# Encoder layer: a third of the adaLN modulation ahead of the projections, the rest during attention

## Chip, core and metric

The kernel runs on one core of one Trainium2 chip. The metric is the device time of one execution in microseconds (us), the median of three runs. A profile is one further execution, recorded by the hardware. Engines are named as the profile names them: PE multiplies matrices (PEld loads its weights), DVE is the vector engine, ACT the scalar engine, POOL the general one, SP issues transfers; a "q" behind a name is the queue of that engine, where transfers (DMAs) are issued.

## What is computed

One bidirectional encoder layer over two sequences, a prompt of 256 tokens and a sample of 1024, width 1024. Each sequence has a vector `c`, from which six rows of 1024 are made that shift, scale and gate the two halves of the layer:

```python
mod = jax.nn.silu(c) @ w_ada + b_ada            # w_ada: 1024 x 6144, float32, 24 MB
sh1, sc1, g1, sh2, sc2, g2 = split(mod, 6)
u = layer_norm(x) * (1 + sc1) + sh1             # needs the first third of mod
h = u @ w_in                                    # then two attention groups, 8 + 8 heads
mix = concat(rms(o_a), rms(o_m)) @ w_out
x = layer_norm(alpha * x + g1 * mix, ...)       # from here on: the other two thirds
u2 = layer_norm(x) * (1 + sc2) + sh2
y = layer_norm(alpha * x + g2 * ffn(u2), ...)
```

The products of `mod` are plain float32 matmuls; nearly all others take their operands split into a high and a low part of type fp32r and sum three products (helper `three`, lines 158 to 160).

## The kernel before

Every instruction stands in its engine's stream in an order written out by hand, and engines wait for each other by semaphores. The stages that matter here follow one another:

`modulation` (from line 162). `w_ada` comes in 12 chunks of 512 columns, 2 MB each, into a ring of three (`w_ada_ring`, issued by SP, line 204). PE multiplies each chunk by `silu_c` in 8 steps, with 2 weight columns (one for each sequence), into a PSUM bank (line 224). DVE adds the bias (`mod_chunk`, line 260), and ACT stores the chunk to the DRAM tensor `mod_rows` (line 241). Beside it the projection weights arrive: 11 pieces (8 of `w_in`, 2 of `w_uq`, 1 of `w_ukv`), which POOL loads into a ring of two (`w_raw`, line 213), ACT rounds to the high part (line 238) and DVE subtracts for the low part (`split`, line 250). DVE takes one `split` and one `mod_chunk` in turn, and POOL loads piece m only after the split of piece m - 2.

`projections` is in the same block, so each engine goes on when its own stream allows. SP first waits for the first chunks of `mod_rows` and reads the columns of `sc1` and `sh1` back (`mod_in_t`, line 362), then loads the first two tiles of x and the tables. DVE takes the moments of two tiles (lines 640, 641), adds one to the scale (line 647) and makes `x_hat` (lines 655, 658). ACT and DVE overwrite memory of the stage before only after `after_modulation`: all 11 splits done, and all 12 chunks stored.

`attention` works through 16 heads of 9 units. In each unit PE does the scores of 128 keys against up to 1024 queries (lines 983, 984 for the first 8 heads, three products at 986 to 988 for the others), two matmuls for the maxima of a later head (line 1031) and the value products of the unit two back (`LAG = 2`). ACT takes the exponential (line 1084) and rounds it (line 1088), DVE makes the low part (line 1123) and the maxima (line 1131). The maxima, their transposes and those of the outputs share one pair of PSUM banks, `A_PAIR`, in an order that a list of `uses` numbers: each use waits until DVE has freed the one before (`a_free`). From head 8 on, `w_out` is split into `k.wo` high and low; until then these 64 KB in each partition are empty.

`output` and `channel` (the feed-forward part) read the other thirds of `mod_rows` later, from 838 us on.

Of the kernel before, what the change touches and what calls it, by code (L numbers as in the profile page):

```python
# [27 lines left out]
P = 128  # L28
# [41 lines left out]
class Kernel:  # L70
    def __init__(self, nc, ctx, ins, outs):
        self.nc, self.ctx = nc, ctx
        self.i, self.o = ins, outs
        self.names = set()

    def sem(self, name):
        return self.ctx.enter_context(self.nc.semaphore(name))
# [8 lines left out]
def encoder_layer(nc, ins, outs):  # L86
    ctx = ExitStack()
    with ctx:
# [3 lines left out]
        k.eps = k.sb(ctx, "eps", [P, 1])  # L92

# [13 lines left out]
        k.o_sample = lambda t: outs["y_sample"][0, t * P:(t + 1) * P, :]  # L107
        with ExitStack() as weights:
            k.win = [k.sb(weights, f"w_in_{s}", [P, KT, W_IN], F32R) for s in ("hi", "lo")]
            k.wuq = [k.sb(weights, f"w_uq_{s}", [P, RQ // P, HM * DM], F32R) for s in ("hi", "lo")]  # L110
            k.wukv = [k.sb(weights, f"w_ukv_{s}", [P, HM * (NOPE + VD)], F32R) for s in ("hi", "lo")]
            with nc.Block() as block, ExitStack() as early:
                k.early = early
                with ExitStack() as stage:
                    modulation(k, stage, block)
                with ExitStack() as stage:
                    projections(k, stage, block)
        k.u2_memory = ctx.enter_context(ExitStack())
        with ExitStack() as weights:
            w_out_lo_memory = weights.enter_context(ExitStack())  # L120
            k.wo = [k.sb(weights, "w_out_hi", [P, KT, D], F32R), k.sb(w_out_lo_memory, "w_out_lo", [P, KT, D], F32R)]
            with ExitStack() as stage:
                attention(k, stage)

            k.u2 = [k.sb(k.u2_memory, f"u2_{s}", [P, KT, TOK], F32R, side="right") for s in ("hi", "lo")]
# [38 lines left out]
def modulation(k, stage, block):  # L164
# [4 lines left out]
    NC = 6 * D // 512  # L169
    RING = 3  # L170
    right = lambda name, shape: k.sb(stage, name, shape, side="right")
    c_t = right("c_t", [P, KT, 2])
    silu_c = right("silu_c", [P, KT, 2])
    wa = right("w_ada_ring", [P, RING, KT, 512])
    bias = right("b_ada_rows", [2, 6 * D])
    mrow = right("mod_chunk", [2, 2, 512])
    raw = right("w_raw", [P, 2, W_IN])
    c_in, ident_in = k.sem("c_in"), k.sem("ident_in")
    wa_in = [k.sem(f"wa_in{s}") for s in range(RING)]
    b_in = k.sem("b_ada_in")  # L180
    raw_in = [k.sem(f"raw_in{s}") for s in range(2)]
    c_ready, mod_done, mod_sum = k.sem("c_ready"), k.sem("mod_done"), k.sem("mod_sum")
    mod_out = [k.sem(f"mod_out{s}") for s in range(2)]
# [7 lines left out]
    k.mod_out, k.lo_done, k.pieces = mod_out, lo_done, len(pieces)  # L191
    k.ident_in, k.eps_ready = ident_in, k.sem("eps_ready")

    @block.sync
    def _(sp):
# [4 lines left out]
        wsrc = k.i["w_ada"][0].rearrange("(p j) n -> p j n", j=KT)  # L200
        for n in range(NC):
            if n >= RING:
                sp.wait_ge(mod_done, n - RING + 1)
            sp.dma_start(wa[:, n % RING, :, :], wsrc[:, :, n * 512:(n + 1) * 512]).then_inc(wa_in[n % RING], 16)

    @block.gpsimd
    def _(pool):
        pool.memset(k.eps[:, :], EPS).then_inc(k.eps_ready, 1)
        pool.dma_start(k.ident[:, :], k.i["ident"]).then_inc(ident_in, 16)
# [6 lines left out]
    @block.tensor  # L216
    def _(pe):
        pe.wait_ge(c_ready, 1)
        for n in range(NC):
            pe.wait_ge(wa_in[n % RING], 16 * (n // RING + 1))  # L220
            if n >= 8:
                pe.wait_ge(mod_sum, n - 7)
            for j in range(KT):
                mm = pe.matmul(bank(k, n % 8)[0:2, :], silu_c[:, j, :], wa[:, n % RING, j, :],  # L224
                               start=j == 0, stop=j == KT - 1)
            mm.then_inc(mod_done, 1)

    @block.scalar
    def _(act):
        act.dma_start(bias[:, :], k.i["b_ada"][0, :].partition_broadcast(2)).then_inc(b_in, 16)  # L230
        act.wait_ge(c_in, 32)
        act.activation(silu_c[:, :, :], c_t[:, :, :], ACT.Silu).then_inc(c_ready, 1)
        assert len(pieces) <= NC
        for n in range(NC):
            if n < len(pieces):
                act.wait_ge(raw_in[n % 2], 16 * (n // 2 + 1))
                hi = pieces[n][1]
                act.activation(hi, raw[:, n % 2, :hi.shape[-1]], ACT.Copy).then_inc(hi_done, 1)
            if n >= 1:
                act.wait_ge(mod_sum, n)  # L240
                act.dma_start(k.mod[:, (n - 1) * 512:n * 512], mrow[:, (n - 1) % 2, :]).then_inc(mod_out[(n - 1) % 2], 16)
        act.wait_ge(mod_sum, NC)
        act.dma_start(k.mod[:, (NC - 1) * 512:], mrow[:, (NC - 1) % 2, :]).then_inc(mod_out[(NC - 1) % 2], 16)

    @block.vector
    def _(dve):
# [4 lines left out]

        for n in range(NC):
            if n < len(pieces):
# [4 lines left out]
            if n >= 2:  # L258
                dve.wait_ge(mod_out[n % 2], 16 * (n // 2))
            dve.tensor_tensor(mrow[:, n % 2, :], bank(k, n % 8)[0:2, :], bias[:, n * 512:(n + 1) * 512], ALU.add).then_inc(mod_sum, 1)  # L260
        for m in range(NC, len(pieces)):
# [4 lines left out]
def projections(k, stage, block):  # L266
# [54 lines left out]
    tabs_in, mod_in, modp = k.sem("tabs_in"), k.sem("mod_in"), k.sem("mod_plus_one")  # L321
# [34 lines left out]
    def _(sp):  # L356
        for s in range(2):
            sp.wait_ge(k.mod_out[s], 32)
        with nc.allow_non_contiguous_dma(reason="modulation columns, once"):
            for s in range(2):  # L360
                for m, part in enumerate((1, 0)):
# [116 lines left out]
    def _(act):  # L478
# [22 lines left out]
        for n in TURNS:  # L501
            a, b, c = n - 1, n - 3, n - 4
            if n < NT:
                if n == 0:
                    act.wait_ge(modp, 1)
# [118 lines left out]
    def _(dve):  # L624
# [20 lines left out]
        dve.wait_ge(mod_in, 64)  # L645
        for s in range(2):
            m = dve.tensor_scalar(modt[:, s, 0, :], modt[:, s, 0, :], 1.0, None, ALU.add)
            if s == 0:
                link(m)
        m.then_inc(modp, 1)  # L650
# [112 lines left out]
def attention(k, stage):  # L763
# [31 lines left out]

    q_in, k_in, v_in = ([k.sem(f"{n}{s}") for s in range(RING)] for n in ("q_in", "k_in", "v_in"))
# [44 lines left out]
    for g in range(H):  # L841
        for u in range(UNITS):
# [4 lines left out]
            if beside(g, u):  # L847
                uses.append(("item", *beside(g, u)))
    uses.append(("outputs", H - 1))
# [8 lines left out]
    def out_use(g):  # L858
        return number["outputs", g]

# [56 lines left out]
    with nc.Block() as block:  # L917
        @block.sync
        def _(sp):
            load_first(sp)  # L920

            for g in range(H):
                sp.wait_ge(m_row, g + 1)
                row = qs[1][DA:DA + 1, g % RING, :] if gqa(g) else qs[0][DM:DM + 1, g % RING, :]
                sp.dma_start(row.bitcast(F32), mrow[:, :].bitcast(F32)).then_inc(m_in, 16)

        @block.gpsimd
        def _(pool):
# [21 lines left out]
            with nc.allow_non_contiguous_dma(reason="columns of gains, once"):  # L950
                for m, name in enumerate(("grp_norm_a", "grp_norm_b")):
                    pool.dma_start(gain[:, 4 * m:4 * m + 4], k.i[name][0, :].rearrange("(j p) -> p j", p=P)).then_inc(gain_in, 16)
            for g in range(H):
# [9 lines left out]
        def _(pe):  # L963
# [81 lines left out]

            for i in range(ITEMS):
# [4 lines left out]
            for g in range(H):  # L1051
                for u in range(UNITS):
# [15 lines left out]
                    if beside(g, u) and twice:  # L1068
                        maxima(*beside(g, u))
            for u in range(UNITS - LAG, UNITS):  # L1070
# [4 lines left out]
        def _(act):  # L1075
# [24 lines left out]
            def w_out_hi(j):  # L1100

                act.wait_ge(gain_in, 32)
                act.wait_ge(wo_in, 16 * (j + 1))
                act.activation(k.wo[0][:, j, :], wo_raw[:, :], ACT.Copy, scale=gain[:, j:j + 1]).then_inc(wo_hi, 1)

            for g in range(H):
                for u in range(UNITS):
                    exp(g, u)
                    if u == 1 and g >= 1:
# [8 lines left out]
        def _(dve):  # L1118
# [39 lines left out]

            for i in range(ITEMS):
# [4 lines left out]
            for g in range(H):  # L1164
                for u in range(UNITS):
# [7 lines left out]
                    if beside(g, u):  # L1173
                        maximum(*beside(g, u))
                    if u == 8 and g >= HA:
# [762 lines left out]
```

## Time and profile before

| | |
|---|---|
| median of three runs | 1982.06 us (1980.81 to 1983.81) |
| profiled execution | 1981.43 us, its span from first to last instruction 1979.6 us |
| PE busy | 1807.0 us, 91% |
| DVE busy | 1163.6 us, 59% |
| ACT busy | 697.9 us, 35% |
| modulation | to 98.8 us |
| projections | about 99 to 364 us |
| attention | 364 to about 820 us |

Busy shares over the span average stages with different limits, so each stage is read by itself below. The end of a matmul is modelled in the records, and a matmul's record overlaps the next one's; what it costs in a stream is the distance between two starts. A plain float32 matmul leaves two records, so 96 instructions of line 224 are x192.

### The profile page before, as it was taken

Reading aid. Unit: us, or ns where it says so; the run is one execution under the profiler, and the core shown is the slowest. Engines: PE = TensorE matmul, PEld = TensorE weight load, DVE = VectorE, ACT = ScalarE, POOL = GpSimd, SP = SyncE. Lnnn points to the kernel's source line nnn. Section 1 sums busy time; section 2 is a strip of 40 time slices with the busy share of each in tenths; the row PEclk is TensorE's granted clock in tenths of the full one; section 3 lists DMA queues with packets and bytes.
Section 4 is the critical chain, followed back from the end, with each engine's and each line's share of the span. In section 5 each row is a group of like instructions: output and inputs, shape, how many; then the busy total and the mean of one; then the engine's idle time right before and its main releaser. Section 6 shows DMA issues by size and latency. Waiting matters only on the chain. (4 is left out here: it accounts for less than half of the span.)

```text
span 1979.6 us, 22389 instructions
## 1 busy us (share of the span) xinstructions
PE 1807.0 (91%) x8558; PEld 1395.8 (71%) x8558; DVE 1163.6 (59%) x1406; ACT 697.9 (35%) x1081; POOL 210.2 (11%) x218
## 2 busy tenths in 40 slices
PE   7989896399999999679979999999999999999993
PEld 1188885266667777467768888888888888888873
DVE  1268887488887777359854434434444434444488
ACT  1145654277776766534431111111111111111114
POOL 0012333111022221000000000000000000000053
PEclk9989997699999999889989999999999999999997
DMA  9913435713155543143241111111111111111133
GB/s 348 323 57 91 133 108 157 173 46 77 46 120 135 123 105 80 47 138 107 75 128 32 33 42 32 32 53 32 32 42 32 32 53 32 32 42 32 34 105 128
DMA packets 145001, 171.56 MB, mean 87 GB/s; under 512 B 21434, under 2 KB 108506, under 8 KB 144930
## 3 DMA queue, kind: packets, MB, share of 16 engines
q1 hardware_dynamic: 130352, 121.72, 19.7%
q0 software_dynamic: 12016, 46.22, 9.3%
q10 hardware_dynamic: 2564, 2.72, 0.5%
q8 instruction: 42, 0.69, 0.1%
q14 instruction: 27, 0.22, 0.0%
HBM read 128.22 MB, written 42.32 MB: 86 GB/s over the span
## 5 line engine op out<-in xcount | busy, mean ns | idle before, releaser
L1796 DVE TENSOR_TENSOR sum_f<-pair,sum_f 128x1024 f32<-128x1024 f32 x200 | 244.1, 1221 | 468.5 <-PE pair L160 466.8
L158 PE MATMUL pair<-u_hi,w_out_hi 128*128 128x512 f32 (+1 forms) x1056 | 377.0, 357 | 12.2 <-DVE w_out_hi L1424 12.2
L160 PE MATMUL pair<-u_hi,w_out_hi 128*128 128x512 f32 (+1 forms) x1056 | 374.9, 355 | 0.0
L159 PE MATMUL pair<-u_lo,w_out_hi 128*128 128x512 f32 (+1 forms) x1056 | 372.4, 353 | 0.0
L1644 ACT ACTIVATE silu_gate<-pair 128x512 f32<-128x512 f32 (+1 forms) x63 | 33.2, 526 | 574.9 <-PE pair L160 574.9
L158 PEld LDWEIGHTS pair<-u_hi,w_out_hi 128*128 128x128 f32 x1056 | 199.1, 189 | 40.0 <-DVE w_out_hi L1424 12.4
L160 PEld LDWEIGHTS pair<-u_hi,w_out_hi 128*128 128x128 f32 x1056 | 199.0, 188 | 31.1
L159 PEld LDWEIGHTS pair<-u_lo,w_out_hi 128*128 128x128 f32 x1056 | 198.7, 188 | 30.4
L1123 DVE TENSOR_TENSOR p_lo<-p_f,p_hi 128x1024 fp32r<-128x1024 f32 (+1 forms) x144 | 167.2, 1162 | 43.4 <-ACT p_hi L1088 42.9
L158 PE MATMUL pair<-down_hi,hidden_hi 128*128 128x512 f32 x440 | 183.2, 416 | 9.6 <-DVEq L1767 6.1
L1084 ACT ACTIVATE p_f<-pair 128x1024 f32<-128x1024 f32 (+1 forms) x144 | 140.6, 977 | 141.9 <-PE pair L984 69.4
L1131 DVE TENSOR_REDUCE max_col<-pair 128x1 f32<-128x1024 f32 x128 | 155.7, 1221 | 57.3 <-PE pair L1031 57.2
L160 PE MATMUL pair<-down_hi,hidden_lo 128*128 128x512 f32 x440 | 173.5, 394 | 0.0
L159 PE MATMUL pair<-down_lo,hidden_hi 128*128 128x512 f32 x440 | 172.6, 392 | 0.0
L1088 ACT ACTIVATE p_hi<-p_f 128x1024 fp32r<-128x1024 f32 (+1 forms) x144 | 145.8, 1012 | 4.6
L1536 POOL TENSOR_TENSOR sum_f<-sum_f,gate 128x1024 f32<-128x1024 f32 x10 | 29.9, 3015 | 878.3 <-DVE sum_f L1796 878.3
L158 PEld LDWEIGHTS pair<-down_hi,hidden_hi 128*128 128x128 f32 x440 | 82.9, 188 | 56.1 <-DVE sum_f L1796 33.0
L1031 PE MATMUL pair<-k_a,q_a 128*128 128x512 f32 (+3 forms) x288 | 94.2, 412 | 29.7 <-DMA k_a<-ka_t_hi_rows 20.9
L158 PE MATMUL pair<-p_hi,v_hi 128*65 128x512 f32 (+1 forms) x288 | 111.7, 388 | 2.5 <-ACT o_t L1095 1.0
L159 PE MATMUL pair<-p_lo,v_hi 128*65 128x512 f32 (+1 forms) x288 | 109.7, 381 | 0.0
L160 PE MATMUL pair<-p_hi,v_lo 128*65 128x512 f32 (+1 forms) x288 | 109.7, 381 | 0.0
L224 PE MATMUL pair<-w_ada_ring,silu_c 128*2 128x512 f32 x192 | 84.3, 602 | 14.5 <-DMA w_ada_ring<-in_w_ada 14.5
(236 smaller groups left out, 2935.0 us busy)
## 6 DMA issues: line engine op xcount, KB each, us to landing
w_ada_ring<-in_w_ada SPq DMA_DIRECT2D x12, 2048.0 KB, 12.5
gate_up_raw<-in_w_gate SPq DMA_DIRECT2D x21, 512.0 KB, 4.0
gate_up_raw<-in_w_up SPq DMA_DIRECT2D x21, 512.0 KB, 5.2
down_raw<-in_w_down SPq DMA_DIRECT2D x21, 512.0 KB, 3.2
o<-o_head POOLq DMA_DIRECT2D x16, 320.0 KB, 3.6
o_tile<-o SPq DMA_DIRECT2D x10, 512.0 KB, 4.1
x<-y SPq DMA_DIRECT2D x10, 512.0 KB, 2.6
gate_up_raw<-x SPq DMA_DIRECT2D x10, 512.0 KB, 3.6
```

What stands on the lines that cost most here:

```text
L158: pe.matmul(out, a[0], b[0], start=start, stop=False)
L159: pe.matmul(out, a[0], b[1], start=False, stop=False)
L160: return pe.matmul(out, a[1], b[0], start=False, stop=stop)
L224: mm = pe.matmul(bank(k, n % 8)[0:2, :], silu_c[:, j, :], wa[:, n % RING, j, :], start=j == 0, stop=j == KT - 1)
L1031: mm = pe.matmul(dst, qs[0][0:w, s, q], ks[0][0:w, n, key], start=True, stop=True)
L1084: act.activation(pf[:, c % PS, 0:w], src, ACT.Exp, scale=scale).then_inc(e_done, 1)
L1088: act.activation(ph[0][:, c % PS, 0:w], pf[:, c % PS, 0:w], ACT.Copy).then_inc(p_hi, 1)
L1123: dve.tensor_tensor(ph[1][:, c % PS, 0:w], pf[:, c % PS, 0:w], ph[0][:, c % PS, 0:w], ALU.subtract).then_inc(p_lo, 1)
L1131: dve.reduce_max(mcol[:, NTP + i:NTP + i + 1], a_pair(m)[:, :, :].rearrange("p a b -> p (a b)"), AX.X).then_inc(a_free, 1)
L1536: pool.tensor_tensor(sumf[:, t, :], sumf[:, t, :], g2[:, int(t >= NTP), :], ALU.mult).then_inc(gated, 1)
L1644: act.activation(sg[:, 0:hi - lo], k.bank[(slot + c + 1) % 2][:, 0, 0:hi - lo], ACT.Silu).then_inc(silu_done, 1)
L1796: dve.tensor_tensor(sumf[:, t, :], src, sumf[:, t, :], ALU.add).then_inc(dn_added, 1)
```

## The change

1. `modulation` keeps 4 of the 12 chunks (`NC = 2 * D // 512`), each with its own buffer. SP issues chunks 0 and 1, then the first two tiles of x, then chunks 2 and 3, then the tables.
2. The columns of `sc1` and `sh1` no longer go through DRAM. PE transposes each finished chunk, four pieces of 2x128 into bank 7 (`columns`), one chunk behind the products; DVE copies them to `modt`, adding one to the scale. `after_modulation` waits for the splits and for these two copies.
3. DVE does up to three splits ahead of each chunk's sum: 0 to 2, sum 0, 3 to 5, sum 1, 6 to 8, sum 2, 9 and 10, sum 3. ACT rounds the 11 pieces without stores in between.
4. The other 4096 columns come during attention in 16 loads of 1 MB that ACT issues, one in every third unit (heads 0 to 2, then late in head 3 to head 5), into the empty memory of `k.wo`. In unit 2 of head 3 and unit 2 of head 7 PE does 32 plain float32 matmuls each (`modulate_late`), with 32 weight columns (2 of `silu_c` and 30 zeros); the four blocks of 512 columns go to the four groups of 32 PSUM partitions of one bank. DVE adds the bias in one instruction, SP stores the rows.
5. POOL adds a memset and 8 small loads of the bias at the start of attention. SP clears the semaphores of the first two stages (63 by my count) at the start of attention, behind its first loads.

```diff
@@ modulation, SP, PE and DVE
-        for n in range(NC):
-            if n >= RING:
-                sp.wait_ge(mod_done, n - RING + 1)
-            sp.dma_start(wa[:, n % RING, :, :], wsrc[:, :, n * 512:(n + 1) * 512]).then_inc(wa_in[n % RING], 16)
+        for n in range(2):
+            load_first(sp, n)
+        def columns(n):
+            pe.wait_ge(mod_sum, n + 1)
+            for q in range(4):
+                at = 2 * (4 * n + q)
+                mm = pe.transpose(bank(k, 7)[:, at:at + 2], mrow[:, n, q * P:(q + 1) * P], k.ident[0:2, 0:2])
+            mm.then_inc(k.mod_tr, 1)
...
+            if n >= 1:
+                columns(n - 1)
+        columns(NC - 1)
+        done = 0
         for n in range(NC):
-            if n < len(pieces):
-                split(n)
+            for m in range(done, min(done + 3, len(pieces))):
+                split(m)
+            done += 3
             dve.wait_ge(mod_done, n + 1)
@@ projections, waits, SP and DVE
         eng.wait_ge(k.lo_done, k.pieces)
-        for s in range(2):
-            eng.wait_ge(k.mod_out[s], 16 * (6 * D // 512 // 2))
+        eng.wait_ge(modp, 2)
-                    sp.dma_start(modt[:, s, m, :], k.mod[s, part * D:(part + 1) * D].rearrange("(j p) -> p j", p=P)).then_inc(mod_in, 16)
         for t in range(2):
             sp.dma_start(xt[:, t, :], xrow(k, t)).then_inc(x_in[t], 16)
+        for n in (2, 3):
+            k.load_w_ada(sp, n)
+        dve.wait_ge(k.mod_tr, 4)
+        cols = bank(k, 7)[:, 0:4 * KT].rearrange("p (m j s) -> p m s j", m=2, s=2)
+        dve.tensor_copy(modt[:, :, 1, :], cols[:, 0, :, :]).then_inc(modp, 1)
+        dve.tensor_scalar(modt[:, :, 0, :], cols[:, 1, :, :], 1.0, None, ALU.add).then_inc(modp, 1)
@@ attention
+    LATE_AT = {(3, 2): 0, (7, 2): 1}
+    LATE_LOADS = {}
+    for half, (g0, u0) in enumerate(((0, 2), (3, 5))):
+        for j in range(KT):
+            c = g0 * 9 + u0 + 3 * j
+            LATE_LOADS[c // 9, c % 9] = (half, j)
...
+            for done in k.first:
+                sp.sem_clear(done)
...
+            def modulate_late(half):
+                use_before(pe, late_use(half))
+                pe.wait_ge(late_in, 16 * KT * (half + 1))
+                for j in range(KT):
+                    for q in range(4):
+                        mm = pe.matmul(A_PAIR[32 * q:32 * q + 32, 0, :], k.silu_c[:, j, :], late_w[:, j, q * 512:(q + 1) * 512],
+                                       start=j == 0, stop=j == KT - 1)
+                mm.then_inc(a_ready, 1)
...
+            def load_late(half, j):
+                if half == 1:
+                    act.wait_ge(a_ready, late_use(0) + 1)
+                at = FIRST + HALF * half
+                act.dma_start(late_w[:, j, :], k.wada[:, j, at:at + HALF]).then_inc(late_in, 16)
...
+            def late_sum(half):
+                dve.wait_ge(a_ready, late_use(half) + 1)
+                dve.wait_ge(late_b_in, 16 * 8)
+                dve.tensor_tensor(late_row[:, half, :], A_PAIR[:, 0, :], late_bias[:, half, :], ALU.add).then_inc(a_free, 1)
```

## Rows read from the trace of the kernel before

**Rows 1.** Busy time by stretch; columns as in the first line, clock and DMA share last.
```profile
core 0: us, PE busy (x) PEld busy (x) DVE busy (x) ACT busy (x) POOL busy (x), PEclk, DMA share, GB/s
2.00:98.70 96.70, 84.23 (x192) 16.42 (x192) 20.80 (x22) 12.98 (x13) 5.87 (x12) 1.00 0.97 343
40.00:80.00 40.00, 40.00 (x94) 7.89 (x93) 10.99 (x12) 6.44 (x6) 2.68 (x5) 1.00 1.03 386
104.00:120.00 16.00, 13.63 (x63) 12.46 (x63) 7.75 (x13) 8.89 (x21) 0.00 (x0) 0.70 0.29 100
385.00:565.00 180.00, 173.35 (x796) 118.47 (x795) 146.56 (x155) 127.46 (x141) 23.24 (x35) 0.97 0.29 65
590.00:791.00 201.00, 200.25 (x954) 143.97 (x953) 159.82 (x167) 139.60 (x153) 41.85 (x63) 1.00 0.45 109
```

**Rows 2.** The modulation products: group by line, first and last records, and DVE's sums.
```profile
L224 PE MATMUL pair<-w_ada_ring,silu_c 128*2 128x512 f32 x192 | 84.3, 602 | 14.5 <-DMA w_ada_ring<-in_w_ada 14.5
14.47 45.69 PE L224 MATMUL pair<-w_ada_ring,silu_c 128*2 128x512 f32 x102 [14.47 <-DMA w_ada_ring<-in_w_ada]
17.84 0.13 PEld L224 LDWEIGHTS pair<-w_ada_ring,silu_c 128*2 128x2 f32 x1 [0.73 <-issue]
23.29 0.68 DVE L260 TENSOR_TENSOR mod_chunk<-pair,b_ada_rows 2x512 f32<-2x512 f32 x1 [13.19 <-PE pair L224]
30.16 0.68 DVE L260 TENSOR_TENSOR mod_chunk<-pair,b_ada_rows 2x512 f32<-2x512 f32 x1 [4.89 <-PE pair L224]
```

**Rows 3.** The path of a weight piece, in order of time: POOL's load, ACT, DVE.
```profile
2.00 1.07 POOL L213 DMA_DIRECT2D w_raw<-in_w_in  x2
7.51 1.17 ACT L238 ACTIVATE w_in_hi<-w_raw 128x1184 fp32r<-128x1184 f32 x1
8.71 1.39 DVE L250 TENSOR_TENSOR w_in_lo<-w_raw,w_in_hi 128x1184 fp32r<-128x1184 f32 x1 [8.71 <-ACT w_in_hi L238]
25.57 0.53 POOL L213 DMA_DIRECT2D w_raw<-in_w_in  x1 [14.63 <-DVE w_in_lo L250]
33.33 1.19 ACT L238 ACTIVATE w_in_hi<-w_raw 128x1184 fp32r<-128x1184 f32 x1 [7.84 <-DMA w_raw<-in_w_in]
66.77 0.54 POOL L213 DMA_DIRECT2D w_raw<-in_w_uq  x1 [6.33 <-DVE w_in_lo L250]
72.80 0.84 ACT L238 ACTIVATE w_uq_hi<-w_raw 128x768 fp32r<-128x768 f32 x1 [6.08 <-DMA w_raw<-in_w_uq]
73.20 0.54 POOL L213 DMA_DIRECT2D w_raw<-in_w_ukv  x1 [5.89 <-DVE w_uq_lo L250]
80.51 1.06 ACT L238 ACTIVATE w_ukv_hi<-w_raw 128x1024 fp32r<-128x1024 f32 x1 [6.86 <-DMA w_raw<-in_w_ukv]
85.70 1.20 DVE L250 TENSOR_TENSOR w_ukv_lo<-w_raw,w_ukv_hi 128x1024 fp32r<-128x1024 f32 x1
```

**Rows 4.** From the last chunk to the first projection product, in order of time.
```profile
98.83 0.68 DVE L260 TENSOR_TENSOR mod_chunk<-pair,b_ada_rows 2x512 f32<-2x512 f32 x1 [6.19 <-PE pair L224]
100.99 1.37 DVE L640 BATCH_NORM_STATS2 x_stats<-x_tile 128x6 f32<-128x512 f32 x2
102.78 0.16 DVE L655 RECIPROCAL x_std<-x_std 128x1 f32<-128x1 f32 x1
110.45 0.69 PE L158 MATMUL pair<-w_in_hi,u_hi 128*128 128x384 f32 x1 [1.23 <-DVE u_lo L744]
```

**Rows 5.** PE's groups in heads 0 to 7 (390 to 565 us); last: idle before, by releaser.
```profile
L983 PE MATMUL pair<-q_a,k_a 128*128 128x512 f32 (+1 forms) x124 | 48.3, 392 | 0.0
L1031 PE MATMUL pair<-k_a,q_a 128*128 128x512 f32 (+2 forms) x124 | 40.4, 408 | 4.5 <-DVE max_col L1131 4.1
```

**Rows 6.** SP from the start of attention, in order of time; last, 8 issues merged.
```profile
368.71 5.43 SPq L915 DMA_DIRECT2D v_lo<-va_lo_rows  x1
384.24 180.31 SPq L925 DMA_DIRECT2D q_b<-neg_max_row  x8
```

**Rows 7.** Prices of an issue and of a register move on a queue: min, median, max ns.
```profile
L1334 ACTq DMA_DIRECT2D gate_up_raw<-in_w_up x1: 596/596/596, 994.5 to 994.5; - x1
L241 ACTq DMA_DIRECT2D mod_rows<-mod_chunk x11: 229/230/246, 24.0 to 92.7; - x11
L1507 SPq MOVE gate_up_raw<-in_w_gate x20: 29/29/35, 1033.6 to 1837.0; - x20
```

**Rows 8.** Who waited for whom in attention, 385 to 565 us: total, times, longest.
```profile
POOL q_a L883 <- PE pair L984: 76.5, 6, 42.2
ACT p_f L1084 <- PE pair L984: 60.6, 42, 25.9
DVE p_lo L1123 <- ACT p_hi L1088: 13.3, 26, 1.0
```

**Rows 9.** DVE's maxima in heads 0 to 7, 385 to 565 us; columns as in rows 5.
```profile
L1131 DVE TENSOR_REDUCE max_col<-pair 128x1 f32<-128x1024 f32 x57 | 69.6, 1221 | 16.7 <-PE pair L1031 16.6
```

More of the change, by code:

```diff
@@ L73, in __init__ @@
         self.i, self.o = ins, outs
-        self.names = set()
+        self.sems, self.first = ctx, []
     def sem(self, name):
-        return self.ctx.enter_context(self.nc.semaphore(name))
+        found = self.sems.enter_context(self.nc.semaphore(name))
+        if self.sems is not self.ctx:
+            self.first.append(found)
+        return found
     def sb(self, stage, name, shape, dt=F32, side=None):
@@ L189, in modulation, with load_first @@
     pieces += [(k.i["w_ukv"][0], k.wukv[0][:, :], k.wukv[1][:, :])]
-    k.mod_out, k.lo_done, k.pieces = mod_out, lo_done, len(pieces)
+    k.lo_done, k.pieces = lo_done, len(pieces)
     k.ident_in, k.eps_ready = ident_in, k.sem("eps_ready")
+    k.wada = k.i["w_ada"][0].rearrange("(p j) n -> p j n", j=KT)
+    def load_first(sp, n):
+        sp.dma_start(wa[:, n, :, :], k.wada[:, :, n * 512:(n + 1) * 512]).then_inc(wa_in[n], 16)
+    k.load_w_ada = load_first
     @block.sync
@@ L208, in _ @@
         pool.memset(k.eps[:, :], EPS).then_inc(k.eps_ready, 1)
+        pool.memset(k.silu_c[:, :, :], 0.0).then_inc(c_zero, 1)
         pool.dma_start(k.ident[:, :], k.i["ident"]).then_inc(ident_in, 16)
@@ L217, in _ @@
     def _(pe):
+        def columns(n):
[4 more added lines that the diff above has]
+            mm.then_inc(k.mod_tr, 1)
         pe.wait_ge(c_ready, 1)
+        pe.wait_ge(ident_in, 16)
         for n in range(NC):
-            pe.wait_ge(wa_in[n % RING], 16 * (n // RING + 1))
-            if n >= 8:
-                pe.wait_ge(mod_sum, n - 7)
+            pe.wait_ge(wa_in[n], 16)
             for j in range(KT):
-                mm = pe.matmul(bank(k, n % 8)[0:2, :], silu_c[:, j, :], wa[:, n % RING, j, :],
-                               start=j == 0, stop=j == KT - 1)
+                mm = pe.matmul(bank(k, n)[0:2, :], k.silu_c[:, j, 0:2], wa[:, n, j, :], start=j == 0, stop=j == KT - 1)
             mm.then_inc(mod_done, 1)
+            if n >= 1:
+                columns(n - 1)
+        columns(NC - 1)
     @block.scalar
     def _(act):
-        act.dma_start(bias[:, :], k.i["b_ada"][0, :].partition_broadcast(2)).then_inc(b_in, 16)
+        act.dma_start(bias[:, :], k.i["b_ada"][0, 0:2 * D].partition_broadcast(2)).then_inc(b_in, 16)
         act.wait_ge(c_in, 32)
-        act.activation(silu_c[:, :, :], c_t[:, :, :], ACT.Silu).then_inc(c_ready, 1)
-        assert len(pieces) <= NC
-        for n in range(NC):
-            if n < len(pieces):
[L236 to L243, printed above, removed]
+        act.wait_ge(c_zero, 1)
+        act.activation(k.silu_c[:, :, 0:2], c_t[:, :, :], ACT.Silu).then_inc(c_ready, 1)
+        for n, (src, hi, lo) in enumerate(pieces):
+            act.wait_ge(raw_in[n % 2], 16 * (n // 2 + 1))
+            act.activation(hi, raw[:, n % 2, :hi.shape[-1]], ACT.Copy).then_inc(hi_done, 1)
     @block.vector
@@ L257, in _ @@
                 dve.wait_ge(b_in, 16)
[L258 to L261, printed above, removed]
+            dve.tensor_tensor(mrow[:, n, :], bank(k, n)[0:2, :], bias[:, n * 512:(n + 1) * 512], ALU.add).then_inc(mod_sum, 1)
+        for m in range(done, len(pieces)):
             split(m)
@@ L859, in out_use, with late_use @@
         return number["outputs", g]
+    def late_use(half):
+        return number["late", half]
     def a_pair(m):
@@ L925, in _ @@
                 sp.dma_start(row.bitcast(F32), mrow[:, :].bitcast(F32)).then_inc(m_in, 16)
+                for (late_g, _), half in LATE_AT.items():
+                    if late_g == g:
+                        sp.wait_ge(a_free, late_use(half) + 1)
+                        for q in range(4):
+                            at = FIRST + HALF * half + 512 * q
+                            sp.dma_start(k.mod[:, at:at + 512], late_row[32 * q:32 * q + 2, half, :]).then_inc(late_out, 16)
+            sp.wait_ge(late_out, 16 * 8)
         @block.gpsimd
@@ L952, in _ @@
                     pool.dma_start(gain[:, 4 * m:4 * m + 4], k.i[name][0, :].rearrange("(j p) -> p j", p=P)).then_inc(gain_in, 16)
+            link(pool.memset(late_bias[:, :, :], 0.0))
+            for q in range(4):
+                for half in range(2):
+                    at = FIRST + HALF * half + 512 * q
+                    pool.dma_start(late_bias[32 * q:32 * q + 2, half, :], k.i["b_ada"][0, at:at + 512].partition_broadcast(2)).then_inc(late_b_in, 16)
             for g in range(H):
@@ L1108, in _ @@
                     exp(g, u)
+                    if (g, u) in LATE_LOADS:
+                        load_late(*LATE_LOADS[g, u])
                     if u == 1 and g >= 1:
```

52 lines of the change are left out of this document (28 added, 24 removed).

## The prediction, made before the changed kernel ran

> **What bounds the kernel now.** I read busy time by stretch first, then the order of time at the front, then PE's groups in attention.
>
> The front. Until 98.7 us PE does nothing but the modulation products, 84.2 us of records at a granted clock of 1.00 (2.4 GHz), while the DMA engines are busy 0.97 of the stretch and 1.03 from 40 to 80 us [rows 1]. The reader is to see two resources that are both full: PE needs 30.16 - 23.29 = 6.87 us for a chunk [rows 2], and a chunk of 2.1 MB with a piece of 0.6 MB in 6.87 us is 393 GB/s, about what the stretch moved (386). Projections can't begin before both the weights and the modulation are there; the first product comes at 110.45 us, 11.6 us after the last chunk's sum [rows 4].
>
> Attention. PE is busy 173.4 of 180 us in heads 0 to 7 and 200.3 of 201 us later [rows 1], at a clock of 0.97 to 1.00. Its idle time is small (4.5 us in 175 us before the maxima [rows 5]), and ACT waits for PE more than for anything (60.6 us [rows 8]). So PE bounds attention too: whatever is added to PE's stream there lengthens it nearly one for one. PE is full where the products leave and full where they arrive, so moving them alone is worth nothing: the change gains only if they cost less PE time in attention than the front gets shorter.
>
> **The change part by part.** (a) The front. PE's share falls from 12 chunks to 4: first chunk from 14.47 to 23.29 us (its first records stand 0.86 apart, at the lower clock, the rest 0.43 [rows 2]), then three of 6.87 us, so PE alone would end at 23.3 + 20.6 = 43.9 us. The loads: four chunks and two x tiles are 9.4 MB on SP's queue, and pieces 0 to 6, some 4.2 MB, pass beside them; 13.6 MB at 380 GB/s from about 4 us on lands at 40 us, so the last chunk ends at about 47 us.
>
> The weight pieces take over as the limit. A slot of the ring turns in: issue to ACT's start 7.8 us (25.57 to 33.33), ACT 1.2, DVE 1.4, about 0.3 until the next issue, together 10.7 us with DMA busy and 5.5 + 2.9 = 8.4 us where it is not (2.00 to 7.51) [rows 3]. The w_uq pieces take 6.0 + 0.8 + 0.9 + 0.3 = 8.0, w_ukv 7.3 + 1.1 + 1.2 + 0.3 = 9.9 [rows 3]. Slot 0: split 0 ends at 10.1 us, then 20.5, 31, 41.5 for pieces 2, 4, 6, about 49 for piece 8 and 57 to 59 for piece 10, the last two lower by a microsecond or so each as the chunks are in by then. Slot 1: split 3 waits behind sum 0 and ends at 25.4, piece 5 at 36, 7 at 46, 9 at 54. I take 57 us for split 10. Sum 3 stands behind it on DVE, and sums 1 and 2 behind splits 5 and 8; who waits for them is only PE's transposes, and those of the last chunk are hidden under the moments. From sum 3 the tail is that of before: 98.83 to 102.78 is 3.95 us to the first reciprocal [rows 4], with two small copies (0.3 us) where the two additions were. So the reciprocal comes at 61 us in place of 102.8: **-42 us**. Best case, where every piece lands in 5.5 us, the last chunk decides: 47 + 4 = 51 us, -51; worst, every piece at 7.8 us and one more microsecond of waiting in each: 66 us, -37. The x tiles, 1 MB, cost nothing of their own: they are ahead of chunk 2 but inside the sum of loads. The read-back through DRAM was hidden behind chunks 10 and 11 and is worth nothing here. From the first reciprocal on, projections run as before, with the same dip of the clock (0.70 of 2.4 GHz from 104 to 120 us [rows 1]), since PE idles before them in both.
>
> (b) The products moved into attention. 64 instructions of 512 columns. At the front an instruction costs 6.87 / 8 = 0.859 us at the full clock, in two records 0.43 us apart [rows 2]. No row shows instructions that write different groups of 32 partitions one after another, so I bound them. One behind the other they cost 64 x 0.859 = **+55 us**. Each in its own quarter of the array with nothing shared they cost a quarter, **+13.7 us**. Between them: neighbours overlap, but the two passes of one instruction use the same quarter and, issued in order, hold back what stands behind them. Then the second pass of one runs beside the first pass of the next, and each instruction costs one pass, 0.43 us: **+27.5 us**. I take this one, because rows 2 show the two passes of an instruction always 0.43 us apart, one after the other, and because the order in which they are issued is fixed by the program. A gain below a quarter is excluded: there are four groups.
>
> No row bears on whether the array can do it. The Trainium skill, TensorEngine Tiling (Array Packing), Key Properties, says that different tiles load weights and multiply in parallel, and its table promises up to 4x for 32 columns. The Trainium skill, TensorE: Matmul & The Clock Gate, Measured speedup vs the span model, gives 2.38x for three column tiles (as an estimate, 3.1x for four, 18 us here, a sum of 1961); the same page's section The mechanism says that matmuls start and end strictly in program order, which is what would hold back the second pass. No run shown so far says which.
>
> (c) Around each burst. PE first waits for DVE to free A_PAIR; the value products between hide the maximum's 1.22 us [rows 9]. DVE sits in its wait for the burst with the next low part and maximum queued behind; PE needs that low part only two units on, after scores, maxima and values (a unit is 180.3 / 63 = 2.9 us of PE work, seven heads by nine units [rows 6], against DVE's 0.7 + 1.2 us). ACT starves during the burst, but it isn't the bound. I put 1 us to a burst, **+2 us**; the bounds are 0 and 3 each.
>
> (d) ACT's 16 issues. 0.23 us for a tiny one, 0.60 for 512 KB [rows 7]; with 0.5 us, 8 us of ACT in heads 0 to 5. ACT is busy 127 of 180 us there [rows 1], and a low part is needed two units later, so most hides: **+1 us**, between 0 and 9 (all exposed). The loads add 16 MB in some 150 us (51 units) to a stretch at 65 GB/s and 0.29 busy, far from full; head loads are issued two heads ahead, and POOL's waits there are for PE [rows 8].
>
> (e) At nothing: POOL's memset and 8 small loads (some 6 us, and POOL's next task waits up to 42 us for PE [rows 8]); DVE's two sums of 0.7 us; SP's stores; w_out's later wait, which is over by head 8. SP's 63 clears stand behind its first loads and ahead of the first row of maxima: SP is free from 374.1 to 384.24 us [rows 6] (its row there ends at 368.71 + 5.43), 160 ns for each. The cheapest rows are 29 ns for a move and 230 ns for a small issue [rows 7]: 0 us by the first, 4 by the second; I take 0, as a clear moves no data.
>
> The sum: -42 + 27.5 + 2 + 1 = -11.5 us. The profiled span of 1979.6 becomes 1968.1, with 1.8 us around it 1969.9 (its own time was 1981.43). The median of the runs shown is 0.6 us above that: **1970.5 us**.
>
> **The rivals.** Full overlap: the four groups run side by side, 13.7 us in place of 27.5: 1956.7 us. For it: pass and weight load of another quarter share nothing that a row shows. Against: it needs PE to pass over an instruction that waits.
>
> No overlap, the one that ends slower: the 32-column instructions queue one behind the other like those with 2 columns, each burst is 27.5 us, and PE's full stream in attention is 55 us longer: -42 + 55 + 3 = +16, 1998 us. It decides from the point where an instruction costs more than (42 - 3) / 64 = 0.61 us. For it: every stream of the trace shows starts one behind the other; also that a 2-column product costs the same per column as any. Against: no stream of before has neighbours in different groups, so none could show it. This is also the case in which the change doesn't do what it says, since the work is only moved.
>
> Front not shortened as summed: pieces and clears at their bad ends together (-37, +4, and ACT's +9): 1984.5 with the half overlap, no change.
>
> **How the numbers follow.** Half overlap 0.40, full 0.30, none 0.25, bad ends together 0.05. The range has to reach the none case, since leaving it out leaves more than 2 in 10 out: 1950 (full overlap, front at -49) to 2001 (none, with 3 us of the open costs). The likeliest case's own range is 1961 to 1979. A difference of 0.2%, 4 us, is about what a measurement of this kernel can tell from no change. Faster 0.70, same 0.05, slower 0.25.
>
> **What would show it.** In the profile after: the first `x_hat` at 57 to 66 us, with DVE's last split as what its sum stood behind, and DMA busy near 1.0 until about 40 us; the two bursts in heads 3 and 7 of 13.7 us each (7 for full overlap, 27.5 for none), seen as the distance between the starts of neighbouring records; the rest of attention as long as before, with heads 0 to 5 longer by less than 2 us; the first row of maxima 20 us after attention's start. Wrong would be: a burst that waits for its loads, a front that ends with the chunks and not with the pieces, or a clock that falls around the bursts, which I hold at 1.00 because PE never idles there.

## The result and the profile after

The changed kernel takes 1953.0 us (median of four runs, 1951.4 to 1953.3) against 1981.4 us for the kernel before beside it: a ratio of 0.985, 95% interval 0.983 to 0.986. It is 28 us faster, where 11.5 us was forecast. In the profiled executions the span falls from 1979.6 to 1951.5 us.

Busy time by stretch in the changed kernel (columns as in [rows 1]); the last line but one is heads 0 to 6 (as the line from 385 to 565 us in [rows 1] is), the last is a late part of attention:

```profile
span 1951.5 us, 22479 instructions
PE 1770.9 (91%) x8574; PEld 1391.4 (71%) x8574; DVE 1159.8 (59%) x1400; ACT 699.1 (36%) x1081; POOL 216.0 (11%) x228
0.00:40.00 40.00, 23.23 (x47) 4.35 (x48) 10.93 (x9) 9.83 (x9) 5.53 (x15) 0.96 0.96 351
58.04:75.26 17.22, 13.70 (x55) 12.56 (x56) 8.89 (x16) 9.04 (x22) 0.00 (x0) 0.60 0.26 92
345.00:525.00 180.00, 174.59 (x836) 117.77 (x837) 142.94 (x150) 124.78 (x139) 22.35 (x34) 0.97 0.53 154
550.00:751.00 201.00, 200.25 (x955) 143.49 (x952) 160.34 (x168) 139.75 (x152) 41.97 (x63) 1.00 0.45 109
```

PE does 36 us less in all (1807.0 before), although the same products of the modulation are made. DMA moves 154 GB/s in heads 0 to 6 in place of 65 [rows 1], half busy.

The front of the changed kernel in order of time; these lines answer to [rows 2 to 4]:

```profile
33.89 8.72 PE L242 MATMUL pair<-w_ada_first,silu_c 128*2 128x512 f32 x16 [2.07 <-DMA w_ada_first<-in_w_ada]
42.88 7.03 PE L242 MATMUL pair<-w_ada_first,silu_c 128*2 128x512 f32 x16
51.86 1.06 ACT L256 ACTIVATE w_ukv_hi<-w_raw 128x1024 fp32r<-128x1024 f32 x1 [1.87 <-DMA w_raw<-in_w_ukv]
52.95 1.22 DVE L263 TENSOR_TENSOR w_ukv_lo<-w_raw,w_ukv_hi 128x1024 fp32r<-128x1024 f32 x1 [1.96 <-ACT w_ukv_hi L256]
54.09 0.67 DVE L273 TENSOR_TENSOR mod_chunk<-pair,b_ada_rows 2x512 f32<-2x512 f32 x1
58.04 0.16 DVE L661 RECIPROCAL x_std<-x_std 128x1 f32<-128x1 f32 x1
65.70 0.69 PE L167 MATMUL pair<-w_in_hi,u_hi 128*128 128x384 f32 x1 [1.23 <-DVE u_lo L750]
```

The reader is to see that the product of the last chunk ends at 49.9 us (42.88 + 7.03), but its sum stands behind the last split on DVE, which ends at 54.2 us. The first reciprocal comes at 58.04 us. The last chunk's product stood behind the one before it, which took 8.72 us in place of 6.87: PE had waited 2.07 us for that chunk, and from 33.89 to 37.4 us its granted clock was 0.54. The splits end later still, so this costs nothing here.

A burst in attention, PE's products as one merged line, then the first weight loads (PEld), the next unit's first score and DVE's sum. A float32 product leaves two records, here called its passes, each with a weight load of its own; a quarter is the part of the array that writes one group of 32 PSUM partitions:

```profile
432.50 7.07 PE L1089 MATMUL pair<-w_ada_late,silu_c 128*32 128x512 f32 x64 [0.61 <-DVE max_col L1190]
432.50 0.16 PEld L1089 LDWEIGHTS pair<-w_ada_late,silu_c 128*32 128x32 f32 x8 [0.87 <-DVE max_col L1190]
432.96 0.13 PEld L1089 LDWEIGHTS pair<-w_ada_late,silu_c 128*32 128x32 f32 x4 [0.30 <-issue]
433.39 0.13 PEld L1089 LDWEIGHTS pair<-w_ada_late,silu_c 128*32 128x32 f32 x4 [0.30 <-issue]
439.51 0.50 PE L1021 MATMUL pair<-q_a,k_a 128*128 128x512 f32 x1
439.64 0.69 DVE L1222 TENSOR_TENSOR mod_late<-pair,b_ada_late 128x512 f32<-128x512 f32 x1 [7.20 <-PE pair L1089]
```

64 passes take 7.07 us. Eight weight loads come at the start and then four in each step of 0.43 us, not one: all four quarters of the array are at work. The granted clock is 1.00 throughout. The scores of the next unit begin at 439.51, and DVE's sum 7.2 us after its last work. The second burst, from 543.27 us, takes 7.07 us as well.

SP's issues place the stages: its first load of attention, and the rows of maxima, of which the merged line that begins with head 8's is the last (in the changed kernel the lines between, from head 4 on, are left out). First the kernel before, then the changed one:

```profile
364.34 0.51 SPq L913 DMA_DIRECT2D q_a<-qa_t_hi_rows  x1
589.69 201.99 SPq L925 DMA_DIRECT2D q_a<-neg_max_row  x8
```

```profile
321.19 0.51 SPq L937 DMA_DIRECT2D q_a<-qa_t_hi_rows  x1
341.09 77.21 SPq L951 DMA_DIRECT2D q_b<-neg_max_row  x4
561.69 201.96 SPq L951 DMA_DIRECT2D q_a<-neg_max_row  x8
```

| event | before, us | after, us | difference |
|---|---|---|---|
| first reciprocal | 102.78 | 58.04 | -44.7 |
| attention's first load | 364.34 | 321.19 | -43.15 |
| row of maxima, head 0 | 384.24 | 341.09 | -43.15 |
| row of maxima, head 8 | 589.69 | 561.69 | -28.0 |
| end of the span | 1979.6 | 1951.5 | -28.1 |

So the front gives 44.7 us, projections lose 1.6 of them, heads 0 to 7 lose 15.15, and nothing changes behind head 8.

### The profile page after: what moved, and what is told of

It is laid out like the page before. It is cut to its first block and busy times, and to the rows that moved or that the text cites. A ratio compares the mean times of both kernels' runs of the same rounds, so it can differ in the third digit from the quotient of the medians.

```text
span 1951.5 us, 22479 instructions
## 1 busy us (share of the span) xinstructions
PE 1770.9 (91%) x8574; PEld 1391.4 (71%) x8574; DVE 1159.8 (59%) x1400; ACT 699.1 (36%) x1081; POOL 216.0 (11%) x228
## 5 line engine op out<-in xcount | busy, mean ns | idle before, releaser
L169 PEld LDWEIGHTS pair<-down_hi,hidden_lo 128*128 128x128 f32 x440 | 82.8, 188 | 20.0
```

The lines of the kernel that those rows point to most:

```text
L169: return pe.matmul(out, a[1], b[0], start=False, stop=stop)
```

## The experiments

The question was why 64 products cost so little, so the first runs change only the order and the place of the late products. All runs below whose number of executions isn't given were timed in one execution; the kernel before, beside them, took 1981.6 us (four products in a row, 64 loads: 1981.9). Theory A was that of the prediction (issued in order, a product whose quarter is busy holds back all behind it), theory B that PE looks past it.

**All products of one quarter, then the next.**

```diff
-                for j in range(KT):
-                    for q in range(4):
+                for q in range(4):
+                    for j in range(KT):
```

> The 32 products of a burst in another order: all eight of one group of 32 PSUM partitions, then all eight of the next. Nothing else is changed and the result is the same. Theory A (issued in order, and a product whose quarter is busy holds back all behind it): neighbours in the stream share a quarter in 28 of 31 places, so a burst goes from 7.1 us to about 27 us and the span from 1951.5 to about 1992 us. Theory B (PE looks past a product that waits for its quarter, at least over some instructions): the burst stays near 7 us if it looks past 8 instructions, and lies between if it looks past fewer.

Measured: 1983.2 us, a span of 1981.4. The burst in order of time, and three of its weight loads:

```profile
431.09 22.59 PE L1089 MATMUL pair<-w_ada_late,silu_c 128*32 128x512 f32 x64 [0.61 <-DVE max_col L1190]
435.84 0.11 PEld L1089 LDWEIGHTS pair<-w_ada_late,silu_c 128*32 128x32 f32 x1 [0.32 <-issue]
436.27 0.14 PEld L1089 LDWEIGHTS pair<-w_ada_late,silu_c 128*32 128x32 f32 x3 [0.32 <-issue]
436.70 0.14 PEld L1089 LDWEIGHTS pair<-w_ada_late,silu_c 128*32 128x32 f32 x2 [0.29 <-issue]
```

22.6 us is neither 27 nor 7. The first quarter has 16 passes; 12 steps after the start (431.09 + 12 x 0.43 = 436.25) the loads become three and then two: the next quarter has begun, four passes before the first is through. Weight loads can stand ahead of their passes (eight at the start of the burst shown above, where four passes begin), so the loads alone would not prove it; the length of the burst does, 52.5 steps for 64 passes. PE looks ahead, but not far. The whole gain of the late products hangs on their order: in this one the changed kernel takes as long as the kernel before.

**Two products of a quarter in a row.** The loops are now over pairs of `j`, the quarter, and `j` within the pair.

> The 32 products of a burst with two of the same quarter in a row before the next quarter, result unchanged. Theory A (in order, a product whose quarter is busy holds back all behind it): of the four passes of a pair, only the last runs beside the next quarter's first, three passes of 0.43 us for a pair, 16 pairs, about 20 us for a burst and a span of about 1977 us. Theory B (PE looks past waiting products): 7 us and 1951.5 us.

Measured: 1951.5 us, a burst of 7.14 us. Theory A, by which four passes of one quarter in a row hold back the next, falls: it gave 20 us. The records show four passes begun within the first step (431.0 to 431.4 us), where the first four of the stream are all of one quarter. Since passes of one quarter take 0.43 us each one after another (the run with all products in one quarter, below), passes of other quarters must here have begun ahead of earlier ones that waited.

**Two weight columns in place of 32.**

```diff
-                        mm = pe.matmul(A_PAIR[32 * q:32 * q + 32, 0, :], k.silu_c[:, j, :], ...
+                        mm = pe.matmul(A_PAIR[32 * q:32 * q + 2, 0, :], k.silu_c[:, j, 0:2], ...
```

> The weights of the late products are 2 columns in place of 32 (the 30 zeros left out), in the same four groups of partitions. If the overlap comes from the group of partitions alone, the burst stays at 7.1 us and the span at 1951.5 us. If it needs 32 full columns, a burst takes 27.5 us and the span is about 1992 us.

Measured: 1955.6 us, a burst of 7.05 us. The overlap comes from the group of partitions; the 30 columns of zeros are not needed for it. Up to head 8 this run is as fast as the changed kernel (that row of maxima comes at 560.94 us); its span is 2.3 us longer, all of it behind that, where the two kernels do the same, so I don't put it down to the edit. Why this execution was longer there is not shown.

**All products in one quarter.**

```diff
-                        mm = pe.matmul(A_PAIR[32 * q:32 * q + 32, 0, :], ...
+                        mm = pe.matmul(A_PAIR[0:32, q % 2, :], ...
```

The `start` and `stop` marks are moved too, so that two groups of columns share a bank; these lines are left out here.

> All late products write partitions 0 to 31 (into two banks in turn), so that no two of them use different quarters; two thirds of the modulation are therefore not what they should be. Both theories: no overlap, 0.86 us for a product, 27.5 us for a burst, a span of about 1992 us, slower than the kernel before by 12 us. If the span stays near 1951.5, it isn't the quarters that make the burst short.

Measured: 1994.5 us, a span of 1992.7, a burst of 27.65 us:

```profile
431.13 27.65 PE L1089 MATMUL pair<-w_ada_late,silu_c 128*32 128x512 f32 x64 [0.61 <-DVE max_col L1190]
```

This is the rival without overlap, built: the change without its four groups would be slower than the kernel before by some 13 us. Four quarters make a burst 27.65 / 7.07 = 3.9 times shorter.

**Four products of a quarter in a row.** From the three orders so far (the change's, two and eight in a row) I fitted a rule: a pass begins once the pass four places ahead of it in the stream has begun and its own quarter is free. It gives 16 steps for the change's order and for two in a row, and 52 for eight in a row (52 x 0.43 = 22.4). The run was chosen because the rule had to say something new.

> Four products of a quarter in a row (eight passes), then four of the next, result unchanged. From the two orders run so far I take that PE begins a pass at most four passes ahead of the one that waits: eight products in a row took 22.6 us (52.6 steps of 0.43), two in a row 7.1. By that rule a quarter begins 4 steps after the one before, the second round too, so 36 steps: 15.5 us for a burst and a span of about 1968 us. If PE looked past eight passes it would be about 7 to 9 us (1953 us); if it looked past none, 24 us (1985 us).

Measured: 1970.6 us, a burst of 15.85 us against 15.5 by the rule, a span of 1968.8 against 1968. The rule held where it could have failed. It isn't the only one that fits: if each quarter takes up to four passes, the running one with them, and PE hands them out in order until one is full, the five orders need the same 16, 16, 36, 52 and 64 steps. The runs can't tell the two apart, and what in PE makes it four is not shown.

**Price of the products in place.** Of each burst only the first 4 of 32 products are left.

> Each late burst does only its first 4 of 32 products (28 left out, so two thirds of the modulation are wrong); loads, sums, stores and waits stay. It prices the products in place. A burst falls from 7.1 to about 0.9 us. If the products cost PE's stream their own length and nothing else, the time falls by 2 x 6.0 = 12 us from that of the changed kernel, to about 1941 us; if their neighbourhood (stalls behind them, a fall of the clock) costs more, by up to 18 us.

Measured: 1940.4 us (median of four; ratio to before 0.979, interval 0.977 to 0.980). From attention's first load to the row of head 8 it is 549.19 - 320.68 = 228.5 us, against 240.5 in the changed kernel and 225.35 before. So 56 products cost 12.0 us, 0.214 each, a quarter of 0.859, and nothing around them. Of the 15.15 us of heads 0 to 7, 13.7 are products; 1.4 are all the rest: two waits of 0.61 and 0.65 us for the maximum and what little else there is.

**Price of the loads.** In addition to the short bursts 14 of the 16 loads are left out (the wait for them is lowered to match; that line is left out here).

```diff
-        for j in range(KT):
+        for j in range(1):
             c = g0 * 9 + u0 + 3 * j
```

> As the run with short bursts, and 14 of the 16 loads during attention are left out too (what they bring is not used there). It prices ACT's issues, 0.33 us each in the profile of the changed kernel, and their 14 MB. If all is hidden, as theory has it, the time is that of the run with short bursts, 1941 us. If the issues are exposed, it is 14 x 0.33 = 4.7 us lower, 1936 us.

Measured: 1940.7 us (median of four), within 0.4 us of the run with the loads, and 548.82 - 320.12 = 228.7 us over the same stretch. The loads and their issues cost nothing that can be measured.

**64 loads of 256 KB.** How many issues can ACT's stream take?

> The 16 late loads of 1 MB cut into 64 of 256 KB, four issued by ACT in a row at the same places; result unchanged. ACT issues 48 more, some 16 us in heads 0 to 5, in lumps of 1.3 us. If there is room for them in ACT's stream, the span stays at 1951.5 us within 1; if the lumps reach PE through the low parts, it is up to 16 us longer, 1967 us.

Measured: 1956.1 us; from attention's first load to the row of head 8 244.7 us, 4.2 more than in the changed kernel. Who waited for whom on PE shows where:

```profile
PE pair L167 <- DVE p_lo L1184: 4.3, 4, 1.1
```

The line is of the stretch from 340 to 520 us (total, times, longest); in the same stretch of the changed kernel this wait doesn't appear. Four issues in a row in ACT's stream delay a rounding so far that PE's value products wait for the low part, four times for about a microsecond; the other lumps are hidden. One issue at a time, which took 0.33 us, has room.

The last runs ask what ends the front, and go beyond the change. The changed kernel was timed again beside the first two.

> The changed kernel itself, timed beside the next two: 1953 us, 0.985 of the kernel before.

Measured: 1952.3 us (median of five, as in all runs from here on), ratio 0.984 (0.983 to 0.986).

**The moments first.**

```diff
         moments(0)
         moments(1)
+        k.last_turn()
         dve.wait_ge(k.mod_tr, 4)
```

`k.last_turn` does splits 9 and 10 and sum 3; the loop that it is taken out of is left out here.

> The moments of the first two x tiles (3.3 us of DVE) stand behind sum 2 and ahead of splits 9 and 10 and sum 3, where DVE waits for pieces, in place of behind sum 3. If the front ends with the weight pieces and the tail behind them, the first reciprocal comes about 2.5 us sooner, at 55.5 us, and the time falls by 2 to 3 us, to about 1950.5 us. If something else ends it (the table load of ACT, the product of the last chunk), nothing moves.

Measured: 1950.0 us (ratio to before 0.983, interval 0.982 to 0.985). The first reciprocal comes at 53.91 us, where the changed kernel run beside it has 57.08. The intervals of the two ratios overlap; what the trace shows beyond doubt is the 3.2 us at the reciprocal.

**A third buffer for the pieces.**

```diff
+    third = k.xh[:, :, :].rearrange("p a b -> p (a b)")
+    def slot(m, w):
+        return third[:, 0:w] if m % 3 == 2 else raw[:, m % 3, 0:w]
...
-            if m >= 2:
-                pool.wait_ge(lo_done, m - 1)
+            if m >= 3:
+                pool.wait_ge(lo_done, m - 2)
```

> As the run with the moments first, and the weight pieces have a third buffer (in the memory of x_hat, which is free until then), so that a piece is loaded three ahead. If the ring of two limits the front, as my sum said, split 10 ends at about 49 us in place of 54.2, the last chunk's product at 50 us becomes the limit, and the reciprocal comes at about 52 us, 3 us sooner again: about 1947 us. If DMA bandwidth limits it, the pieces only take from the chunks, the last chunk lands later and little is won: 1950 us.

Measured: 1945.9 us (ratio 0.981, interval 0.980 to 0.982), and 1946.0 when timed again. The front of this run in order of time:

```profile
43.00 7.03 PE L248 MATMUL pair<-w_ada_first,silu_c 128*2 128x512 f32 x16 [1.77 <-DMA w_ada_first<-in_w_ada]
48.86 1.22 DVE L269 TENSOR_TENSOR w_ukv_lo<-w_raw,w_ukv_hi 128x1024 fp32r<-128x1024 f32 x1 [2.32 <-ACT w_ukv_hi L262]
50.07 0.68 DVE L277 TENSOR_TENSOR mod_chunk<-pair,b_ada_rows 2x512 f32<-2x512 f32 x1
51.41 0.15 DVE L668 RECIPROCAL x_std<-x_std 128x1 f32<-128x1 f32 x1
```

The last split (ends at 50.08) and the last product (50.03) now come together, so both limits of the front are met at once. The last chunk lands later than in the changed kernel, at 43.0 us in place of 40.8 (12.8 + 28.0 from issue to landing), and PE waits 1.77 us for it. That fits the expectation's rival, by which the pieces take from the chunks, but they give more than they take. This version beats both kernels: 6.4 us less than the changed one beside it (1952.3), 37.9 less than the kernel before.

**Spare products on PE.** Projections take 263.15 us from the first reciprocal to attention's first load, against 261.56 before. The granted clock of the first 17.2 us is 0.60 where the same stretch of before (102.78 to 120 us) has 0.70, and PE had idled from 49.9 to 59.2 us but for two groups of small transposes; before the change it idled 5.2 us. This run tests whether that is the cause.

```diff
         columns(NC - 1)
+        pe.wait_ge(lo_done, len(pieces))
+        k.keep_busy(pe, 8)
...
+                if n < 2:
+                    k.keep_busy(pe, 4 + 4 * n)
```

> As the run with three pieces, and PE does 20 spare fp32r products of 384 columns (into a bank that nobody reads) where it idles before the first projection products: 8 behind the last chunk, 4 and 8 behind the transposes of the first two tiles. In the changed kernel projections took 1.6 us longer from the first reciprocal to the end of the stage than before, beside a longer spell at half clock. If that spell is the cause, and PE's idling brings it, the spell shrinks, the first products come 0.17 us apart in place of 0.32, and the time falls by 1 to 3 us below the 1945.9 us of the run with three pieces. If the spell costs nothing (DVE is the limit there), or the spare products delay the transposes, the time stays or rises by up to 2 us.

> The run with three pieces again, beside the one with the spare products: 1946 us, 0.981 of the kernel before.

Measured: 1945.5 us (0.981, interval 0.980 to 0.983) beside 1946.0 for its base. The stretch from 51 to 64 us, first with the spare products, then without:

```profile
51.00:64.00 13.00, 11.38 (x69) 10.48 (x69) 5.60 (x12) 8.08 (x20) 0.00 (x0) 1.00 0.35 120
```

```profile
51.00:64.00 13.00, 9.27 (x36) 8.09 (x36) 5.73 (x12) 7.81 (x19) 0.00 (x0) 0.61 0.34 117
```

The spell at 1.2 GHz is gone, the first products come 0.17 us apart in place of 0.32, and the stage is 2.4 us shorter (260.4 us against 262.75). Filling PE's idle time thus took the spell away, and the spell is worth 2.0 us in the profile (DVE's `norm_factors` of the first tile come 21.71 us behind the first product with the spare products, 23.75 without); in the timed runs the difference, 0.6 us, can't be told from none.

How much of the 1.6 us is it? At half clock PE runs from the first product on for 3.3 us in the kernel before and for 6.2 us in the changed one, and DVE's `norm_factors` of the first tile come 23.17 and 24.47 us behind the first product. Until DVE's last but one `latents_t_hi` 1.0 us of this is left (210.06 and 211.06 us behind the first product). To the last one it takes 15.6 us before and 16.7 in the changed kernel, and there the clock is at work a second time, at the transposes and the six `w_ukv` products of a late tile. First the kernel before, then the changed one:

```profile
330.64 0.66 PE L418 MATMUL pair<-ident,kv_mla 128*128 128x128 f32 x4 [2.27 <-ACT qm_tr L580]
336.13 1.15 DVE L682 CAST latents_t_hi<-latents_t 128x384 fp32r<-128x384 f32 x1 [1.17 <-ACT latents_t L549]
```

```profile
286.90 1.12 PE L426 MATMUL pair<-ident,kv_mla 128*128 128x128 f32 x4 [2.83 <-ACT qm_tr L588]
293.49 1.15 DVE L688 CAST latents_t_hi<-latents_t 128x384 fp32r<-128x384 f32 x1 [2.29 <-ACT latents_t L557]
```

The granted clock over that PE work is 0.75 before (330.6 to 333.5 us) and 0.55 in the changed kernel (286.9 to 290.6), and DVE's `latents_t_hi` comes 5.5 and 6.6 us behind its start. DVE's wait for `q_mla` behind it is 0.4 us shorter in the changed kernel (4.39 against 4.82): 1.0 + 1.1 - 0.4 is the 1.6. The run with three pieces, whose spell at the first products is shorter (full clock from 63.1 us, 4.6 after the first of them), loses 0.4 and 1.2 us in the same two places; its first product comes 0.4 us sooner behind the reciprocal, so that its stage is 1.2 us longer than before. Why the clock stands lower at the late tile isn't shown; no run bears on it.

## Why the prediction was right and wrong

**The front (a)** was right in mechanism and 2.7 us too cautious: 44.7 us at the first reciprocal where 42 was said. The order of events is the one written: the last chunk in at 40.8 us (40 was said), its product done at 49.9 (47 was said; the half clock in the product before it, which it stood behind, was in no term), then the weight pieces, then the tail of 3.95 us (54.09 to 58.04, exactly that of before). The mis-sized term is the last split, at 54.2 us and not 57: the w_in pieces behind the first two took 6.2 to 7.1 us from issue to ACT's start, where I had counted 7.8, and the last three 5.3, 3.4 and 4.3 us. The run with a third buffer shows that the ring was the limit: the last split ends 3.1 us sooner than in the changed kernel timed beside it (50.08 and 53.2).

**The products (b)** are the step that failed. The bounds held, 13.7 and 55 us, and the value taken between them, 27.5, was wrong; the measured one is the lower end. I reasoned that two passes of one product must follow each other, and that PE, issuing in order, would hold back what stands behind the second. The first half is true (one quarter alone: 27.65 us for a burst). The second isn't: PE begins passes of other quarters ahead of one that waits, over four places by the rule above, so that 64 products cost 13.7 us and not 27.5. The order of the change needs less than that. [rows 2], on which I rested it, show a stream in one quarter only; they could not bear on the question, and the middle value had no more behind it than the lower one.

The Trainium skill, TensorE: Matmul & The Clock Gate, The mechanism, says that matmuls keep strict program order in start and end, which is the order that my middle value assumed. The bursts contradict it as it stands: with two products of a quarter in a row, 16 steps for 64 passes are possible only if later passes of other quarters begin before earlier ones that wait. The Trainium skill, TensorEngine Tiling (Array Packing), Theoretical Speedup, gives up to 4x for 32 columns, and here it is 3.9x for plain float32.

**Around the bursts (c)**: 2 us said, 1.4 measured. **ACT's issues (d)**: 1 us said, none measured, with an issue at 0.33 us and not the 0.5 I took. The run with 64 loads shows that issues can reach PE: sixteen single ones don't, four in a row do. **At nothing (e)**: held; attention's first load and its first row of maxima are 19.9 us apart in both kernels, so the 63 clears on SP are hidden.

The sum with the terms as measured: -44.7 + 1.6 + 13.7 + 1.4 = -28.0 us. The projections' 1.6 us was in no term; I had said that the stage runs as before, with the same dip of the clock. The dip was longer. The rival of the bad ends was added up 3 us too low: 5, 4 and 8 us on top of 1970.5 are 1987.5, which is 5 us slower than before and not "no change". The full overlap rival, at 1956.7 us, with a chance of 0.30, came within 4 us of the result; its sum of -25.3 us lacked 2.8, the front's 2.7 us, while the two other differences (1.6 us less around the bursts and issues, 1.6 us more in projections) cancel. The rival without overlap is what the change is with all products in one quarter (1994.5 us); in the order of eight in a row (1983.2 us) the gain is gone too.

## What to carry to other kernels

A product with few weight columns that is moved into a full stage of PE pays only if it gets cheaper there: put independent products into the four groups of 32 output partitions and interleave them, so that no quarter has more than two float32 products in a row; here that is the difference between 7.1 and 22.6 us for the same 32 products. Where no row of a trace bears on a bound, the middle has no more behind it than the ends: say what decides between them, and forecast from there. And where two queues of work meet at the end of a stage, look at what stands between them on the engine that joins them: moving 3.3 us of moments ahead of a wait brought the reciprocal forward by nearly all of it.

## What the hardware showed that I had not expected

Plain float32 products in four groups of output partitions run fully side by side: 0.214 us each for 512 columns in place of 0.859. Two weight columns are as good as 32 for this (7.05 and 7.07 us for a burst). PE starts passes out of program order, over a reach of four passes: the fitted rule gave 15.5 us for an order that then took 15.85. Spare products in PE's idle time kept the granted clock at 1.00 in place of 0.61 and made the projections 2.4 us shorter in the profile.
